# Down products of the two layers: ten panels of a half's 32 in seven block products, two in each odd group of four

## The reference

```
hn = rmsnorm(h, g)                                    # [256, 2048]
ff = jnp.square(jax.nn.relu(hn @ w_up)) @ w_down      # 2048 -> 8192 -> 2048
h  = h + rmsnorm-scaled ff                            # residual
```

## Time and profile before

| | |
|---|---|
| median of 3 runs | 3261.73 us (3261.12 to 3262.33) |
| the profiled execution's own time | 3262.3 us |
| its span, first to last instruction | 3260.5 us |
| TensorE matmul busy | 3236.0 us (99%), 17237 instructions |
| VectorE busy | 2180.9 us (67%) |
| ScalarE busy | 1568.1 us (48%) |
| DMA read | 594.86 MB, 183 GB/s over the span |
| mean granted TensorE clock | 0.999 of full speed |

### The profile page before, as it was taken

One profiled execution on the slowest core, in us unless ns is written; L12 is line 12 of the kernel. 1 busy time (PEld: TensorE's weight loads), 2 busy tenths in 40 slices (PEclk: granted clock), 3 DMA queues, 4 the chain that ended last, 5 costly groups with the idle time before them and its releaser, 6 DMA issues.

```text
span 3260.5 us, 45588 instructions
## 1 busy us (share of the span) xinstructions
PE 3236.0 (99%) x17237; PEld 2792.2 (86%) x17237; DVE 2180.9 (67%) x2584; ACT 1568.1 (48%) x1830; POOL 267.8 (8%) x211
## 2 busy tenths in 40 slices
PE   8999999999999999999999999999999999999999
PEld 8999888888888888888888888888888888888887
DVE  7888665557865656565555688875656555568887
ACT  5336453445554544544434455554454534445555
POOL 6422000000000024000000000001400000000000
PEclk9999999999999999999999999999999999999999
DMA  7544565555665555455555566655545565556564
GB/s 211 163 134 155 194 200 187 193 185 189 206 194 193 165 178 181 142 181 181 187 190 190 186 200 200 200 178 176 183 150 175 192 193 189 184 189 198 195 204 155
DMA packets 249327, 598.65 MB, mean 184 GB/s; under 512 B 22296, under 2 KB 64248, under 8 KB 248184
## 3 DMA queue, kind: packets, MB, share of 16 engines
q1 hardware_dynamic: 248056, 591.17, 56.2%
q0 software_dynamic: 768, 5.24, 0.4%
q10 hardware_dynamic: 384, 0.58, 0.0%
HBM read 594.86 MB, written 2.10 MB: 183 GB/s over the span
## 4 chain that ended last, share of the span: by engine, by line
PE 96%; DVE 2%; ACT 1%; DVEq 0%; DMA 0%; issue 0%; SPq 0%; ACTq 0%
PE ps L1167 26%; PE ps L682 21%; PE ps L1422 18%; PE ps L688 11%; PE ps L1119 5%; PE ps L1070 3%; PE ps L756 2%; PE ps L764 2%; PE ps L757 2%; PE ps L1479 1%; PE ps L625 1%; PE ps L1474 1%; DVE wlo L2295 1%; PE ps L1316 0%; PE ps L1314 0%; DMA x<-in_x 0%
## 5 line engine op out<-in xcount | busy, mean ns | idle before, releaser
L2295 DVE TENSOR_TENSOR wlo<-raw,whi 128x2048 fp32r<-128x2048 f32 (+1 forms) x425 | 971.2, 2286 | 571.7 <-ACT whi L1592 571.2
L1592 ACT CAST whi<-raw 128x2048 fp32r<-128x2048 f32 x425 | 805.6, 1896 | 495.5 <-PE ps L688 426.9
L682 PE MATMUL ps<-xT,whi 128*128 128x512 f32 x3072 | 733.5, 391 | 1.4 <-DVE xT L2313 1.1
L682 PEld LDWEIGHTS ps<-xT,whi 128*128 128x128 f32 x3072 | 564.6, 188 | 111.5 <-issue 1.3
L1167 PE MATMUL ps<-whi,stage 128*128 128x512 f32 x2480 | 593.3, 389 | 0.0
L1167 PEld LDWEIGHTS ps<-whi,stage 128*128 128x128 f32 x2480 | 465.2, 188 | 96.3
L1422 PE MATMUL ps<-whi,xT 128*128 128x512 f32 (+1 forms) x1792 | 444.2, 388 | 1.1 <-DVE wlo L2998 0.9
L688 PEld LDWEIGHTS ps<-xT,wlo 128*128 128x128 f32 x3072 | 393.9, 191 | 15.0
L688 PE MATMUL ps<-xT,wlo 128*128 128x256 f32 x3072 | 398.5, 283 | 0.0
L2998 DVE TENSOR_TENSOR wlo<-raw,whi 128x2048 fp32r<-128x2048 f32 (+3 forms) x126 | 275.8, 2189 | 171.1 <-ACT whi L2058 171.0
L1422 PEld LDWEIGHTS ps<-whi,xT 128*128 128x128 f32 x1792 | 326.2, 188 | 63.4 <-issue 1.7
(11 more groups left out here) (495 smaller groups left out, 3009.2 us busy)
## 6 DMA issues: line engine op xcount, KB each, us to landing
raw<-in_mlp_w SPq DMA_DIRECT2D x128, 1024.0 KB, 5.1
raw<-in_w_up SPq DMA_DIRECT2D x128, 1024.0 KB, 5.2
raw<-in_w_down SPq DMA_DIRECT2D x128, 1024.0 KB, 5.3
raw<-in_w_in SPq DMA_DIRECT2D x100, 1024.0 KB, 5.1
raw<-in_w_o SPq DMA_DIRECT2D x32, 1024.0 KB, 5.3
raw<-in_w_out SPq DMA_DIRECT2D x16, 1024.0 KB, 5.1
raw<-in_w_in SPq DMA_DIRECT2D x16, 832.0 KB, 4.4
raw<-in_w_uq SPq DMA_DIRECT2D x8, 768.0 KB, 4.4
```

The costliest lines, as they stand in the source:

```text
L682: mm(psum(bank + j), whi[:, u % 2, c:c + P], xT[:, k, :], start=k == 0, stop=False)
L1592: act.copy(whi[:, u % 2, 0:width], raw[:, u, 0:width]).then_inc(sig["hi"], 1)
L2295: tt(wlo[:, u % 2, 0:width], raw[:, u, 0:width], whi[:, u % 2, 0:width].bitcast(F32), SUB).then_inc(sig["lo"], 1)
```

## The change

In `down7`, groups 1, 3 and 5 take panels u = 0 and u = 2 in seven products; groups 0, 2, 4 and 6 take u = 2 alone as before, and group 7 none. A half has 10 panels in seven products instead of 7. The groups behind group 0 are now three pairs of an odd and an even group: the engines loop over pairs (VectorE and TensorE write the last pair out).

VectorE makes the sums for a panel u = 2 after its part of panel u = 0 of that group, as before (with a drain ahead where u = 0 is itself in seven products, since the sums' buffers are reused). The sums for a panel u = 0 of an odd group are made after panel u = 2 of the group before, behind a drain. `down` keeps its order and is written with the same functions. The core of the diff, in the order TensorE (`pe`), ScalarE (`act`), VectorE (`dve`: the pair, then the piece of group 0, then the loop):

```diff
-    down7=dict(quad=16, sth=128, stl=128, done=RT * CHUNKS - 2, tsum=14, xsum=14, xshi=14, xslo=14, hit=14, lot=14, u1=2, uall=2))
+    down7=dict(quad=16, sth=128, stl=128, done=RT * CHUNKS - 2, tsum=20, xsum=20, xshi=20, xslo=20, hit=20, lot=20, u1=2, uall=2))
...
+PAIRS, DENSE = 3, 10
+
+
+def dense(half, pair, place):
+
+    return DENSE * half + 1 + 3 * pair + place
...
+                    def quad(i, sevens, begin=False, end=False):
                         for u in range(4):
+                            if u in sevens:
+                                seven_products(half, Qh + i, sevens[u], u, k0 + 8 * i, begin=begin, end=end and u == 2)
                             else:
                                 panel(half, Qh + i, u, k0 + 8 * i, begin=begin and u == 0)
 
+                    def pair(p, end=False):
+                        quad(2 * p + 1, {0: dense(half, p, 0), 2: dense(half, p, 1)})
+                        quad(2 * p + 2, {2: dense(half, p, 2)}, end=end)
+
+                    if add:
+                        quad(0, {2: DENSE * half}, begin=True)
+                        with pe.Fori(0, PAIRS - 1) as p:
+                            pair(p)
+                        pair(PAIRS - 1, end=True)
...
+                        with act.Fori(0, PAIRS) as p:
+                            for u in range(4):
+                                panel(half, 2 * p + 1, u, dense(half, p, u // 2) if u % 2 == 0 else None)
+                            for u in range(4):
+                                panel(half, 2 * p + 2, u, dense(half, p, 2) if u == 2 else None)
...
+                def pair(half, p, last=False):
+                    for u in range(4):
+                        panel(half, 2 * p + 1, u, dense(half, p, u // 2) if u % 2 == 0 else None)
+                        if u == 0:
+                            dve.drain()
+                            operand_sums(half, 2 * p + 1)
+                    for u in range(4):
+                        panel(half, 2 * p + 2, u, dense(half, p, 2) if u == 2 else None)
+                        if u == 0:
+                            operand_sums(half, 2 * p + 2)
+                        if u == 2 and not last:
+                            dve.drain()
+                            operand_sums(half, 2 * p + 3, 0)
...
+                        if u == 2 and not begun:
+                            dve.drain()
+                            operand_sums(half, 1, 0)
...
+                        with dve.Fori(0, PAIRS - 1) as p:
+                            pair(half, p)
+                        pair(half, PAIRS - 1, last=True)
```

More of the change, by code:

```diff
@@ L1575, in _ @@
                 more = layer + 1 < DEPTH2
-                down("down7", up_at, Y, not more, (0, 1), next_rows if more else None, add=add_ffn)
+                down("down7", up_at, Y, not more, next_rows if more else None, add=add_ffn)
                 st.stage("add_ffn")
@@ L1984, in panel @@
                     for kk in range(2):
-                        n = P if fast and kk == 0 else SEQ
+                        n = P if m is not None and kk == 0 else SEQ
                         act.copy(stage[:, (2 * u + kk) % 4, 0:n], hT[:, bass.ds(k0 + kk, 1), 0:n].rearrange("p o n -> p (o n)"))\
                             .then_inc(sig["sth"], 1)
+                    fast = m is not None
                     if fast:
-                        m = seven(half, i)
                         act.wait_ge(sig["xsum"], at["xsum"] + m + 1)
@@ L1996, in panel, with first_seven @@
                         act.copy(thi, tsum).then_inc(sig["hit"], 1)
+                def first_seven(half):
+                    return None if half and begun else DENSE * half
                 def first_sum(half):
@@ L2004, in down @@
                     for u in range(4):
-                        panel(half, 0, u, half in seven_halves and is_seven(0, u))
+                        panel(half, 0, u, first_seven(half) if u == 2 else None)
                         if half == u == 0:
@@ L2009, in down @@
                             begun(at)
-                    with act.Fori(1, 7) as i:
-                        for u in range(4):
-                            panel(half, i, u, half in seven_halves and is_seven(1, u))
+                    if begun:
+                        with act.Fori(1, 7) as i:
+                            for u in range(4):
+                                panel(half, i, u, i if half == 0 and u == 2 else None)
+                    else:
+                        with act.Fori(0, PAIRS) as p:
[3 more added lines that the diff above has]
+                                panel(half, 2 * p + 2, u, dense(half, p, 2) if u == 2 else None)
                     for u in range(4):
                         panel(half, 7, u)
-                        if u == 0 and half in seven_halves:
+                        if u == 0 and first_seven(half) is not None:
                             first_sum(half)
@@ L2956, in down @@
                                 add(0)
[L2957 to L2961, removed]
+                    if begun:
+                        with dve.Fori(1, 7) as i:
+                            for u in range(4):
+                                panel(half, i, u, i if half == 0 and u == 2 else None)
+                                if u == 0 and half == 0:
+                                    operand_sums(half, i)
+                    else:
+                        with dve.Fori(0, PAIRS - 1) as p:
+                            pair(half, p)
+                        pair(half, PAIRS - 1, last=True)
                     for u in range(4):
                         panel(half, 7, u)
-                        if u == 0 and half in seven_halves:
+                        if u == 0 and first_seven(half) is not None:
                             kept_sums() if begun else sums(half)
@@ L3230, in _ @@
                 more = layer + 1 < DEPTH2
-                add = down("down7", up({3: last_rows}, {3: lambda: norm_scales(ffn, R_FFN, 2)}, Y), Y, ffn_scale, not more, (0, 1),
+                add = down("down7", up({3: last_rows}, {3: lambda: norm_scales(ffn, R_FFN, 2)}, Y), Y, ffn_scale, not more,
                            next_rows if more else None)
```

54 lines of the change are left out of this document (25 added, 29 removed).

## The result

The changed kernel takes 3281.02 us in the median of five runs (3280.27 to 3281.12), the kernel before 3261.73 in the five beside it. The ratio is 1.0058, with a 95% interval of 1.0047 to 1.0069: slower by 19.3 us, where 15 were forecast. The profiled execution's span is 3279.3 us against 3260.5, so 18.8 us of it can be followed in the trace.

What follows compares the result with a forecast made beforehand. TensorE's matmuls were taken to bound the kernel, with VectorE becoming late in places. 8.2 us saved against 23.2 us of waiting gave 15.0 us slower, 3277.3 us from 3262.3 (3277 against the median), range 3268 to 3287.

Steps and rivals of the forecast that it cites:

- The matmuls: TensorE in down7: 12 more panels in seven products remove 36 matmuls at 0.2267 us each, 8.2 us saved.
- The late stretch: VectorE from an even group's panel-2 split through the odd group's panel-1 split: 22.13 us, making TensorE 1.57 us late.
- O1: Panel 1 of a pair's odd group: TensorE about 1.0 us late at its second eight products, 0.4 at its low products.
- E0: Panel 0 of a pair's even group: VectorE waits 1.1 us ahead of its split and is on time there.
- E2: Panel 2 of a pair's even group, in seven products: VectorE on time at its split, about 1.5 us to spare.
- The drain: VectorE, ahead of each new set of operand sums: priced at 0.14 us, with nothing as the least.
- O0: Panel 0 of a pair's odd group, newly in seven products: VectorE's sums 3.56 us, its part as a seven 5.02.
- The first pairs: Group 0 with the odd group behind it, each half: TensorE 2.79 us late in halves 0, 2.51 in halves 1.
- The sum: Over two layers: 23.2 us of TensorE waiting against 8.2 us won, so 15.0 us slower.
- That the matmuls decide: Rival: TensorE stays the fullest engine and at best nothing waits, so 3254.1 us, faster; chance 0.09.
- That only the first pairs are late: Rival: the eight inner pairs lose 0.1 instead of 1.57 us, so 3265.5 us, no change; chance 0.09.
- Code loading: Rival: VectorE's longer loop body costs 0.37 us twice in each of 12 pairs, 8.9 us more, about 3286; chance 0.06.

## Why the prediction was right, and where it was off

**The matmuls.** Right: the plain line has 3432 matmuls after 3720, 288 less, the seven line 252 more, and TensorE has 36 instructions less in all. They are worth what was said: where VectorE is in time, panels follow each other at 4.76 and 5.44 us.

**The late stretch.** Right in its mechanism and place, and nearly in length: 22.39 us against 22.13. TensorE waits ahead of O1's second eight for VectorE's stage and is late at O1's low products behind the split, and VectorE waits 1.07 us at E0, where about 1.1 was said. Less this wait and the 1.12 ahead of E2's split, VectorE's work in a pair is 41.1 us, as the 41 said: the sum fits into the matmuls' 41.48, and TensorE waits even so. Putting 0.8 us into this stretch made every pair 0.70 us longer, putting it elsewhere did nothing, and taking 2.75 us out of it took the loss away.

**The drain.** The mis-sized term. It was priced at 0.14; in the loop the low half and the sums behind it stand 1.93 us apart (1899.39 to 1901.32) where 1.67 would do, 0.26. With two of them in the stretch that is 0.24 of the 0.28 us by which a pair loses more than forecast (1.85 for 1.57). In the last pair of a half, from O0's part on behind the loop, the second drain costs 0.18 and the pair loses 1.64 to 1.66. The prediction's bound for the drain went the other way, to nothing.

**The first pairs.** The first pair of a half loses 2.86 us in both halves 0, where 2.79 was said, and 2.60 and 2.58 in the halves 1, where 2.51 was said.

**GpSimd.** The missed term: 1.8 us in one pair. The argument looked for engines that wait for VectorE and not for one that slows it; the row was there in the trace of before, a split of 4.29 us. That each duration repeats within 1% in all groups, as the prediction says, doesn't hold for that group.

**The sum.** First pairs 10.9, inner pairs 7.4 in the loop and 6.6 behind it, GpSimd 1.8: 26.7 us of waiting, less 8.2, is 18.5 of the 18.8 us in the trace; 23.2 and 15.0 were forecast. The rest is the wait at the end of the last half, 0.4 us, where the prediction had VectorE on time. The measured 3281 lies within the range by its width and not by its terms: the upper bound was made for addresses worked out once more in the loop, and what came on top were GpSimd's products and a dearer drain.

**The rivals.** That the matmuls decide was refuted by the chain, and came closer to true once the sums left the stretch (3257.57) or the sevens stood further apart (3256.45 at best). By TensorE's share of matmuls, 99%, TensorE was the engine to relieve, and 36 matmuls less made the kernel 19 us slower through an engine that is 68% busy. Perfetto Trace Analysis of the Trainium skill (Identifying the Most-Contended Engine) wants TensorE's headroom judged by the matrix work done or by the share of its weight loads, not by its matmul share. Over the whole span the trace doesn't agree even so: the weight loads' 85% still name TensorE. Over the pair alone it agrees: the weight loads take 34.11 of 43.33 us, 79%, VectorE 39.95, 92%. That only the first pairs are late: all pairs are. Code loading: the version without the loop takes the same time with no idle time listed for "issue" in the late stretch, and "issue" ahead of the new sums is 0.18 us in the loop, which is part of the drain's 0.26.

## What to carry to other kernels

An engine that is busy less than the engine that sets the time can still make that engine wait. Where two buffers tie its work to a panel, follow it instruction by instruction from the last place where it waits to the next place where others wait for it. The same work can then cost all of its time, or nothing, by its place alone; so place what is added where there is slack before judging it by its sum, and look again at what every engine beside it did for free while there was slack.

## What the runs showed of the hardware

A drain on VectorE cost 0.26 us between a 128x1536 and a 128x1024 instruction in a loop and 0.18 without one, where the short instructions inside the sums had suggested 0.14. GpSimd's product of 128x512 took 1.28 to 1.30 us at four places between VectorE's instructions (nine sevens at 3, 6, ..., 27), and mostly 3.2 to 4.0 and once 8.4 at the places of the other versions; two of 128x1024 took 6.8 us in one place and 9.41 in another. VectorE's stage pair of 0.76 us took 5.11 beside two products of 128x1024.
